# Three query blocks scored in one run, and the transposes and output products of an attention stage moved between four projections

## The reference

```python
n = _rms(h, norm_mix_w[l])
z = n @ w_in[l]                       # 1024 -> 3*1024 + 2*1024 + 2*1024
q, k, v, glu, g_att, g_conv = jnp.split(z, splits, axis=-1)
# 8 heads, two score maps of width 64 in each, values of width 128
s = jnp.einsum('bqhmd,bkhmd->bhmqk', qb, kb)          # per block of 128 queries
mask = cid[None, :] <= qc[:, None]                    # chunks of 64 keys, 16 meta tokens
p = jax.nn.softmax(jnp.where(mask, s, NEG_INF), axis=-1)
a = p[:, :, 0] - lam * p[:, :, 1]
o = jnp.einsum('bhqk,bkhe->bqhe', a, v)
y_att = _rms(o, subln_w[l]) * (1.0 - lambda_init)
u = causal_dwconv(glu[..., :C] * sigmoid(glu[..., C:]))   # 31 taps
u = silu(layernorm(u)); m = sigmoid(g_att) * y_att + sigmoid(g_conv) * (u @ w_conv_out[l])
```

## Time and profile before

| | us |
|---|---|
| median of 3 runs | 1533.55 (1533.29 to 1533.76) |
| the profiled execution | 1534.0 |
| its span, first to last instruction | 1532.1 |
| TensorE (PE) busy | 1520.7, 99% |
| VectorE (DVE) busy | 1101.7, 72% |
| ScalarE (ACT) busy | 646.7, 42% |
| GpSimd (POOL) busy | 55.4, 4% |

### The profile page before, as it was taken

The page is one execution under the profiler, slowest core; times in us unless marked ns, Lnnn a source line. Parts: engine busy times, 40 slices in busy tenths (PEclk is TensorE's granted clock), DMA queues, the critical chain, the costliest instruction groups (busy, mean ns, idle before and its releaser), DMA issues.

```text
span 1532.1 us, 25451 instructions
## 1 busy us (share of the span) xinstructions
PE 1520.7 (99%) x9994; PEld 1362.9 (89%) x9994; DVE 1101.7 (72%) x1550; ACT 646.7 (42%) x1015; POOL 55.4 (4%) x115
## 2 busy tenths in 40 slices
PE   9999999999999999999999999999999999999998
PEld 8999999999999999999988888878888888888887
DVE  5889888888655587777764458988748887887123
ACT  5224545555643434434334335744645333333122
POOL 0000111111000000000000020000000000000000
PEclk9999999999999999999999999999999999999999
DMA  6333222232233243232232443231132333332221
GB/s 180 83 93 100 56 72 68 57 83 56 56 102 92 83 110 82 82 109 82 66 94 81 115 109 83 57 83 42 56 110 56 110 101 91 89 103 96 110 83 55
DMA packets 235360, 131.64 MB, mean 86 GB/s; under 512 B 20985, under 2 KB 228741, under 8 KB 235285
## 3 DMA queue, kind: packets, MB, share of 16 engines
q1 hardware_dynamic: 234900, 130.40, 30.3%
q0 software_dynamic: 384, 0.20, 0.0%
HBM read 128.48 MB, written 2.10 MB: 85 GB/s over the span
## 4 chain that ended last, share of the span: by engine, by line
PE 91%; DVE 5%; ACT 2%; issue 0%; DMA 0%; SPq 0%; DVEq 0%; ACTq 0%
PE psP L726 32%; PE psS L726 25%; PE psP L791 8%; PE psS L1432 4%; PE psP L1432 4%; PE psP L748 4%; PE psP L1122 3%; PE psP L1300 1%; DVE conv L2170 1%; PE psS L1300 1%; PE psP L969 1%; DVE wl L2050 1%; PE psP L879 1%; PE psS L928 1%; PE psS L1189 1%; PE psP L956 1%
## 5 line engine op out<-in xcount | busy, mean ns | idle before, releaser
L2050 DVE TENSOR_TENSOR wl<-raw,wh 128x2048 fp32r<-128x2048 f32 x124 | 284.1, 2291 | 174.8 <-ACT wh L1487 173.4
L1487 ACT ACTIVATE wh<-raw 128x2048 fp32r<-128x2048 f32 x124 | 237.0, 1911 | 207.1 <-PE psS L1432 74.3
L726 PE MATMUL psP<-xh,wh 128*128 128x264 f32 (+3 forms) x1184 | 296.0, 312 | 1.2 <-DVE wl L2050 0.5
L726 PE MATMUL psP<-xl,wh 128*128 128x264 f32 (+3 forms) x1184 | 291.4, 309 | 0.0
L726 PE MATMUL psP<-xh,wl 128*128 128x264 f32 (+3 forms) x1184 | 290.3, 308 | 0.0
L726 PE MATMUL psS<-xh,wh 128*128 128x256 f32 (+2 forms) x880 | 210.3, 305 | 0.4 <-DVE hT L2079 0.4
L726 PE MATMUL psS<-xl,wh 128*128 128x256 f32 (+2 forms) x880 | 208.1, 303 | 0.0
L726 PE MATMUL psS<-xh,wl 128*128 128x256 f32 (+2 forms) x880 | 207.2, 302 | 0.0
L726 PEld LDWEIGHTS psP<-xh,wh 128*128 128x128 f32 x1184 | 192.2, 189 | 16.3 <-issue 2.2
L726 PEld LDWEIGHTS psP<-xl,wh 128*128 128x128 f32 x1184 | 192.7, 189 | 12.0 <-issue 0.2
L726 PEld LDWEIGHTS psP<-xh,wl 128*128 128x128 f32 x1184 | 192.2, 189 | 11.9
(11 more groups left out here) (483 smaller groups left out, 2429.7 us busy)
## 6 DMA issues: line engine op xcount, KB each, us to landing
raw<-in_w_in_dram SPq DMA_DIRECT2D x74, 512.0 KB, 4.9
raw<-in_w_up_dram SPq DMA_DIRECT2D x44, 512.0 KB, 4.6
raw<-in_ffn_up_dram SPq DMA_DIRECT2D x44, 512.0 KB, 4.9
raw<-in_ffn_down_dram SPq DMA_DIRECT2D x22, 512.0 KB, 3.9
raw<-in_w_out_dram SPq DMA_DIRECT2D x16, 512.0 KB, 4.7
raw<-in_w_down_dram SPq DMA_DIRECT2D x16, 384.0 KB, 3.6
raw<-in_w_down_dram SPq DMA_DIRECT2D x16, 320.0 KB, 4.0
raw<-in_w_conv_out_dram SPq DMA_DIRECT2D x8, 512.0 KB, 4.6
```

Source lines behind the costliest of these rows:

```text
L726: ins = mm(dst, W[:, s, half, k, 0:rows], Y[:, k, c0 + o:c0 + o + w], start=(k == 0 and p == 0), stop=(k == KT - 1 and p == 2))
L1487: fn(wh[:, n % 2], raw[:, n % 2], ACT.Copy).then_inc(s_hi, 1)
L2050: V.tensor_tensor(wl[:, n % 2], raw[:, n % 2], wh[:, n % 2].bitcast(f32), ALU.subtract).then_inc(s_lo, 1)
```

## The change

- `SCORE_COL` and `score_rows`: block 0 keeps columns 0 to 159 of banks 0 and 1, block 1 moves from banks 2 and 3 to columns 160 to 431 of banks 0 and 1, block 2 moves from banks 0 and 1 to banks 2 and 3. `scores(a, 0)` to `scores(a, 2)` follow each other ahead of part 0. Since blocks 0 and 1 now share banks, the maxima of block 0 wait for the scores of block 1, and the exponentials of block 0 wait for the maxima of block 1.
- `turn_back(c)` goes ahead of `probs(b, 3)`, and `gated(c)` ahead of the maxima.
- `outputs(b)` goes behind part 0 in turns 2 to 7. In turns 8 and 9 it stays ahead of part 0. ScalarE's copy and square and VectorE's variances go behind the exponentials and maxima of block 2.
- `values(a)` goes behind part 1 in turns 1 to 7.
- `probs(a, 0)` and `probs(a, 1)` become `first_probs(a)`, three transposes in one go behind `scores(a, 3)`, so s_at and s_ac count four steps for each head where they counted five. ScalarE's normalising of the outputs goes behind its copies.

```diff
@@ TensorE
 def scores(a, t):
-    if a:
-        pe.wait_ge(s_ex, 4 * a + (0, 0, 1, 3)[t])
-    elif t >= 2:
-        pe.wait_ge(s_ex, t - 1 if t == 2 else 3)
+    if t == 3:
+        pe.wait_ge(s_ex, 4 * a + 3)
+    elif a:
+        pe.wait_ge(s_ex, 4 * a)
...
+def first_probs(a):
+    pe.wait_ge(s_cb, 4 * a + 2)
+    pe.wait_ge(s_ac, 4 * a + 1)
+    for j, o in enumerate((PO[0], PO[1], PO[1] + 128)):
+        ins = tr(psP[1][:, 0, 128 * j:128 * (j + 1)], prob[:, o + NM:o + NM + 128], ident[:])
+    ins.then_inc(s_at, 1)
...
 for h in range(NH + 2):
     a, b, c = h - 1, h - 2, h - 3
+    if c >= 0:
+        pe.wait_ge(s_ea, evacuated(2 * (N_HEAD + 2 * h) - 2)[1])
+        turn_back(c, psP[0])
     if b >= 0:
         probs(b, 3)
     if 0 <= a < NH:
         scores(a, 0)
         scores(a, 1)
-    if c >= 0:
-        pe.wait_ge(s_ea, evacuated(2 * (N_HEAD + 2 * h) - 2)[1])
-        turn_back(c, psP[0])
-    if b >= 0:
+        scores(a, 2)
+    if h >= NH:
         outputs(b)
...
     part(h, 0)
-    if 0 <= a < NH:
-        if h < NH:
-            values(a)
-        scores(a, 2)
-        probs(a, 0)
+    if 0 <= b < NH - 2:
+        outputs(b)
...
     part(h, 1)
     if 0 <= a < NH:
-        probs(a, 1)
+        if h < NH:
+            values(a)
         scores(a, 3)
+        first_probs(a)
     part(h, 2)
@@ ScalarE
 def exps(a, t):
-    act.wait_ge(s_ma, 4 * a + t + 1)
+    act.wait_ge(s_ma, 4 * a + max(t, 1) + 1)
@@ VectorE
 def maxima(a, t):
-    dve.wait_ge(s_qk, 4 * a + t + 1)
+    dve.wait_ge(s_qk, 4 * a + max(t, 1) + 1)
@@ VectorE, the loop
+    if c >= 0:
+        gated(c, psP[0])
     if 0 <= a < NH:
         maxima(a, 0)
         maxima(a, 1)
-    if c >= 0:
-        gated(c, psP[0])
...
     taps(4 if h else 8)
     if h == NH:
         clear_sums()
-    if b >= 0:
+    if h >= NH:
         variances(b)
+    if 0 <= a < NH:
+        maxima(a, 2)
     taps(2)
     if h == NH:
         dve.wait_ge(s_lmc, 1)
         centred(0, 4)
-    if 0 <= a < NH:
-        maxima(a, 2)
+    if 0 <= b < NH - 2:
+        variances(b)
```

More of the change, by code:

```diff
@@ L70 @@
 CREDIT = 2
+SCORE_COL = (0, 160, 0)
 BLOCKS = (1, 2, 3, 0)
@@ L491, in row, with score_rows @@
             return t[:, ds(g, 1), c0:c0 + n].rearrange("p o c -> p (o c)")
+        def score_rows(t):
+            o = SCORE_COL[t]
+            return scores_ps[:, 2 * (t // 2):2 * (t // 2) + 2, o:o + PW[t]]
         block = ctx.enter_context(nc.Block())
@@ L643, in meta_probs @@
                 if a and t == 0:
-                    pool.wait_ge(s_at, 5 * (a - 1) + 5)
+                    pool.wait_ge(s_at, 4 * (a - 1) + 4)
                 pool.wait_ge(s_cb, 4 * a + t + 1)
@@ L662, in _ @@
                     if a:
-                        pool.wait_ge(s_at, 5 * (a - 1) + 1)
+                        pool.wait_ge(s_at, 4 * (a - 1) + 1)
                     pool.tensor_copy(vr[:, :, 0:NM], qkv[:, a % 2, 2:3, 0:NM].to_broadcast([128, TT, NM])).then_inc(s_vrp, 1)
@@ L912, in scores @@
             def scores(a, t):
-                if a:
-                    pe.wait_ge(s_ex, 4 * a + (0, 0, 1, 3)[t])
-                elif t >= 2:
-                    pe.wait_ge(s_ex, t - 1 if t == 2 else 3)
+                if t == 3:
+                    pe.wait_ge(s_ex, 4 * a + 3)
+                elif a:
+                    pe.wait_ge(s_ex, 4 * a)
                 if t == 0:
                     pe.wait_ge(s_ea, evacuated(2 * (N_HEAD + 2 * a) + 1)[1])
-                if a and t == 1:
+                if a and t == 2:
                     pe.wait_ge(s_ea, evacuated(2 * (N_HEAD + 2 * a) + 3)[1])
@@ L926, in scores @@
                     if t < 3:
-                        bank = scores_ps[:, 2 * (t % 2) + m, :]
-                        mm(bank[:, 0:PW[t]], q, K[:, 0:PW[t]], start=True, stop=False)
+                        bank = score_rows(t)[:, m, :]
+                        mm(bank, q, K[:, 0:PW[t]], start=True, stop=False)
                         last.append(bank[:, PW[t] - 64:PW[t]])
@@ L952, in probs @@
                 pe.wait_ge(s_cb, 4 * a + t + 1)
-                pe.wait_ge(s_ac, 5 * a + t + 1)
+                pe.wait_ge(s_ac, 4 * a + t)
                 for j in range(t + 1):
@@ L960, in probs @@
                 ins.then_inc(s_at, 1)
+            def first_probs(a):
[4 more added lines that the diff above has]
+                ins.then_inc(s_at, 1)
             def outputs(b):
-                pe.wait_ge(s_ac, 5 * b + 5)
+                pe.wait_ge(s_ac, 4 * b + 4)
                 o = [psP[1][:, 0, 128 * t:128 * (t + 1)] for t in range(TT)]
@@ L1602, in exps @@
                     if t < 3:
-                        src = scores_ps[:, 2 * (t % 2) + m, 0:PW[t]]
+                        src = score_rows(t)[:, m, :]
                     else:
@@ L1614, in copy_values @@
             def copy_values(a):
-                act.wait_ge(s_at, 5 * a + 1)
+                act.wait_ge(s_at, 4 * a + 1)
                 fn(vtok[:], psP[1][:, 0, :].rearrange("p (j e) -> p j e", j=TT), ACT.Copy).then_inc(s_ac, 1)
@@ L1619, in copy_values, with copy_first_probs @@
                 fn(vm[0:32, TT, :], psP[1][0:32, 1, 0:128], ACT.Copy, scale=second[:])
+            def copy_first_probs(a):
+                act.wait_ge(s_at, 4 * a + 2)
+                fn(aT[:, 0, 0:128], psP[1][:, 0, 0:128], ACT.Copy)
+                fn(aT[:, 0:2, 128:256], psP[1][:, 0, 128:384].rearrange("p (j q) -> p j q", j=2), ACT.Copy).then_inc(s_ac, 1)
             def copy_probs(a, t):
-                act.wait_ge(s_at, 5 * a + t + 2)
+                act.wait_ge(s_at, 4 * a + t + 1)
                 ins = fn(aT[:, 0:t + 1, 128 * t:128 * (t + 1)], psP[1][:, 0, 0:128 * (t + 1)].rearrange("p (j q) -> p j q", j=t + 1), ACT.Copy)
@@ L1671, in _ @@
                 if 0 <= a < NH:
-                    if h < NH:
-                        copy_values(a)
                     exps(a, 2)
-                    copy_probs(a, 0)
-                if b >= 0:
+                if 0 <= b < NH - 2:
+                    copy_outputs(b)
+                    square_outputs(b)
+                if h == NH + 1:
                     norm_outputs(b)
@@ L1679, in _ @@
                 if 0 <= a < NH:
-                    copy_probs(a, 1)
+                    if h < NH:
+                        copy_values(a)
+                    copy_first_probs(a)
+                    if b >= 0:
+                        norm_outputs(b)
                     if h == NH:
@@ L2202, in maxima @@
             def maxima(a, t):
-                dve.wait_ge(s_qk, 4 * a + t + 1)
+                dve.wait_ge(s_qk, 4 * a + max(t, 1) + 1)
                 if t < 3:
-                    b = 2 * (t % 2)
-                    ins = V.tensor_reduce(stat[:, 2 * t:2 * t + 2], scores_ps[:, b:b + 2, 0:PW[t]], AX, ALU.max, negate=True)
+                    ins = V.tensor_reduce(stat[:, 2 * t:2 * t + 2], score_rows(t), AX, ALU.max, negate=True)
                 else:
@@ L2227, in combine @@
                     if a:
-                        dve.wait_ge(s_at, 5 * (a - 1) + 5)
+                        dve.wait_ge(s_at, 4 * (a - 1) + 4)
                     V.scalar_tensor_tensor(pm[0:NM, 0, NM:2 * NM], pmeta[:, 1, :], stat[0:NM, 20:21], pmeta[:, 0, :], ALU.mult, ALU.add)
```

## The result

| | us |
|---|---|
| kernel before, median of 22 runs | 1533.69 (1533.29 to 1534.27) |
| changed kernel, median of 22 runs | 1536.47 (1534.78 to 1537.18) |
| ratio | 1.0016, 95% interval 1.001 to 1.0022 |
| profiled execution of the changed kernel | 1536.86, span 1535.1 |

The change costs 2.8 us, where 2.7 had been predicted (1536.2). The total came out by two errors of opposite sign, though, which is luck. The runs of the changed kernel stand in two groups, 8 of them from 1534.78 to 1535.24 and 14 from 1536.23 to 1537.18. The runs before form one group. The profiled execution belongs to the upper group. The medians of the groups are 1534.94 and 1536.86, 1.9 us apart. In what follows one run of e2 (1840.5 us at a mean granted clock of 0.753) is left out.

What follows compares the result with a forecast made beforehand. TensorE, busy 99% of the span, was taken as the bound. Switches -1.2, turn 1 -0.1, turn 8 +3.0 and +0.4, turn 9 +0.6 gave +2.7 us: 1536.2 us, 8-in-10 range 1532.7 to 1539.2.

Steps and rivals of the forecast that it cites:

- Turns 2 to 7 have no wait: In these six turns the new order was to make no new wait on TensorE.
- the limit which the prediction named as a sign of being wrong: The prediction counted as wrong if turns 2 to 7 shortened by more than 0.3 us.
- the switches: Fewer changes between transposes and 64-row scores on TensorE: -0.15 us a head, -1.2 us over 8 heads.
- Turn 1: Old waits of 0.5 and 0.4 us go, a new 0.83 us wait comes ahead of part 1: together -0.1 us.
- VectorE's lateness: VectorE comes into turn 8 late from turn 7, by about 0.4 us (between 0 and 1), all added to turn 8.
- the 1.99 us ahead of the first exponentials: In turn 8 ScalarE's first exponentials start later by 0.60 for turn_back, 0.67 for block 1's scores and 0.72 for its maxima.
- The wait of 1.5 us or more: In turn 8 TensorE was to wait this long behind the copy of the means, ahead of part 0.
- Part 3: In turn 8 its needed exponentials come at T8+31.9 against 32.0 for TensorE: no charge, but no margin.
- A wait of 2.4 us: In turn 8 TensorE was to wait about this long ahead of part 1, on ScalarE's empty(8, 0).
- The ring of VectorE and ScalarE: Rival: their serial chain exceeds TensorE's 32.5 us a turn and becomes the bound, +4.7 us, 1538.2 us; chance 0.23.
- The dear switch: Rival: the switches on TensorE save 0.61 us a head instead of 0.15, -1.0 us in all, 1532.6 us; chance 0.18.
- The fast rival: Rival: turn 8's lateness stays off the path and the switch is dear, -5.0 us, 1528.6 us; chance 0.07.

Runs made afterwards that it cites:

- e2: Changed kernel with only the maxima of block 2 moved back behind the centring in turn 8: 1534.08 us.
- e7: Kernel before with one of turn_back's five transposes moved between the scores of blocks 0 and 1, turns 3 to 8: 1534.61 us.
- e5: Changed kernel with turns 8 and 9 in the old order except first_probs, and head 0's values behind part 0 in turn 1: 1531.81 us.
- e11: Changed kernel with VectorE's last tap and addition moved from turn 7 behind turn 8's first maxima: three runs 1534.49 to 1534.72 us, others 1535.75 to 1536.48.
- e6: Changed kernel with nine unused products filling TensorE's wait ahead of part 1 in turn 8: median 1534.91 us.
- e1: Changed kernel with probs(7, 3) put back ahead of turn_back(6) in turn 9: median 1535.98 us.
- e10: Changed kernel with six unused products ahead of the convolution's means in turn 8, filling only the first long wait: median 1536.68 us.
- e9: Changed kernel with unused products in both long waits of turn 8, six ahead of the means and nine ahead of part 1: median 1535.21 us.
- e3: Changed kernel with head 7's scores in the old banks, block 2 behind part 0 and its maxima behind the centring: 1534.03 us.

## Why the prediction was right, and where it was not

- *Turns 2 to 7 have no wait.* Right. Each is 0.3 us shorter instead of 0.15. That is the limit which the prediction named as a sign of being wrong, and turn 2 is past it (31.83 for 32.19, 0.36 us). The term of the sum that was mis-sized is the return from the 64-row scores to the transposes: I took it as 0 to 0.06 us from one run of transposes (0.60 against 0.54). The loss stood in the scores ahead of it instead: block 1 takes 0.67 us with transposes behind and 0.57 with block 2 behind. That is 0.10 of the 0.30 us. The ten transposes in one go save another 0.05, and the three of `first_probs` take 0.31 (347.17 to 347.48) where their two parts took 0.40 (309.70 to 309.79 and 315.73 to 316.04). With 0.3 for 0.15 the switches save 2.1 us by turn 7, not 1.1. e7 confirms the size (0.23 for one round trip alone).
- *Turn 1.* The wait ahead of part 1 is 0.69 us (predicted 0.83), both old waits are gone. The old wait for the split was larger than its record of 0.50: from block 1's scores to part 0 it was 1.23 us (137.76 to 138.99), where the scores take 0.57 in the changed kernel. That makes -0.48 in all, and e5 gets another 0.54 by covering the new wait.
- *Turn 8.* Part 0 starts 10.20 us and part 1 18.67 us into the turn. Predicted were 10.06 and 18.5, and with VectorE's lateness 10.46 and 18.9. The lateness was put at 0.4 and is 0.45 (e11); the 1.99 us ahead of the first exponentials is 1.76, since `turn_back` costs 0.55, block 1 0.57 and its maxima 0.64 us, for 0.60, 0.67 and 0.72. So the exponentials are 2.20 us later, and then the maxima of block 2 stand ahead of the centring (e2: 0.9). The wait of 1.5 us or more that was to stand behind the copy of the means is split: 1.35 us ahead of the values, on the copied outputs, and 0.43 behind the means. Part 3, put at no charge and no margin, starts 0.18 us late (e6, 390.75 to 391.18). At full clock turn 8 is 3.40 us longer (e6), predicted 3.25. The chain is as described.
- *The clock was left out.* A wait of 2.4 us was predicted, and what TensorE does behind it was not. It costs 1.46 us in the profiled execution. If the upper group is that drop, 14 of 22 executions had it, but this isn't shown (see the last section). That is the second error, with the other sign. At full clock the terms sum to -0.48 -1.82 +3.40 +0.55 = +1.65 us by the profiles, 1.05 less than predicted, and the lower group's median is 1.2 us over the kernel before. The upper group's is 3.2 us over it, just past the 3.1 us line for no change. That line was too wide for these runs: the interval of 1.001 to 1.0022 lies above 1 as a whole. The middle value of 1536.2 agrees with the median because the errors cancelled.
- *The rivals.* The ring of VectorE and ScalarE does come to the bound, but only in turn 7 (0.45 us in turn 8's start) and just in turn 2: in turn 3 the maxima start 2.65 us into the turn without a wait (200.38), 0.1 us behind the 2.56 of the later turns. In turns 4 to 7 VectorE still waits 0.86, 0.40, 0.20 and 0.95 us for the scores. Its slack before was 1.1 us a turn and not 1.3, since the 6.7 us of the earlier trace rows are five waits in six turns. The ring's 31.7 us stands in the prediction without its terms, so only what came of it can be compared. The dear switch fell by e7. The fast rival fell by the waits of turn 8, which stand on ScalarE as the trace before named it.

## What to carry to other kernels

When steps move in a software-pipelined loop, the steady turns are the easy part: walk through the first and last turns separately, since there the step that gave cover (outputs, values, block 2) may be missing or the engine behind it may carry other work. An engine with slack before a change has to be followed around its whole ring afterwards; its last item before the hand-over (here one tap and one addition) can go behind it. A new long wait on TensorE (here 2.45 us) is to be priced twice, once as the wait and once for the clock that may fall behind it (here 1.46 us, in some executions).

## What was not expected of the hardware

The granted clock fell to 0.50 (1.2 GHz of the two levels 1.2 and 2.4) 1.1 us behind the end of a wait of 2.45 us and stayed there for some 3.4 us, though TensorE was busy again. Only one execution of the changed kernel was looked at by stretches. The profiled runs of e1 and e11, both in their upper groups (1535.99 and 1536.16 us), show the drop behind the same wait, and e10's, in the lower one, does not. With both waits filled (e9) no run stands in the upper group. In e3 it fell in part 0 behind waits of 1.49 and 0.43 us. So a shorter wait can do it too. What decides it in one execution and not in the next was not tried.

That the groups are this drop and nothing else isn't shown. They lie 1.9 us apart and the drop costs 1.46. The mean granted clock of the single runs doesn't sort them either: it is 0.998 or 0.999 in both groups of the changed kernel (1.000 or 0.999 in the kernel before), and in e1 0.998 in all three lower runs. So an execution of the lower group may have had a low clock too, at a place where it cost little, as e3's part 0 shows in one profile, or behind the last matmuls, where the kernel before has 0.68 from 1530 to 1532 us.

The Trainium skill ("TensorE: Matmul & The Clock Gate", What's actually happening) says that the slow clock is the resting state and activity lifts it, and the 0.50 behind idle time agrees with this.

The kernels also differ by up to 0.9 us in when turn 1 begins (136.44 to 137.31 us), though nothing ahead of it was changed. Comparisons by turns, from one start to the next, are free of this.
